# The first layer norm and the first two FFN chunks in two halves of 256 tokens

## The reference, cut to what matters

```python
        x = layer_norm(ALPHA * x + y @ w_out[l], ln_mix_g[l], ln_mix_b[l])
        hg, hu = jnp.split(x @ w_ffn_in[l], 2, axis=-1)
        x = layer_norm(ALPHA * x + (jax.nn.silu(hg) * hu) @ w_ffn_out[l], ln_ffn_g[l], ln_ffn_b[l])
```

## Time and profile before

| what | before |
|---|---|
| median of 3 runs | 861.37 us (860.73 to 861.94) |
| the profiled execution, its own time | 860.42 us |
| its span, first to last instruction | 858.6 us |
| TensorE busy | 835.9 us, 97% of the span |
| VectorE, ScalarE, GpSimd busy | 505.4, 347.7, 31.4 us |
| loads | 84.5 MB, 98 GB/s over the span |
| mean granted TensorE clock | 0.992 of full speed |

### The profile page before, as it was taken

How to read it: one execution, slowest core, us unless ns; L and a number is a source line. 1 busy time by engine, 2 the same in 40 slices (tenths; PEclk the granted TensorE clock), 3 DMA queues, 4 the chain that set the end, 5 groups by cost and what they waited for, 6 DMA issues and landing times.

```text
span 858.6 us, 10360 instructions
## 1 busy us (share of the span) xinstructions
PE 835.9 (97%) x3975; PEld 695.9 (81%) x3975; DVE 505.4 (59%) x831; ACT 347.7 (41%) x527; POOL 31.4 (4%) x81
## 2 busy tenths in 40 slices
PE   7999999999999999999999899999999999999995
PEld 4889898888887888888888688888888888888884
DVE  4357888888788987766553686333433333322227
ACT  4545566675645546534341632222222222211112
POOL 2600000000000000000000100000000000000001
PEclk9999999999999999999999999999999999999998
DMA  6552221212121221212253123322222222222202
GB/s 221 172 198 69 80 98 53 95 50 89 59 84 64 98 82 66 97 57 92 98 201 142 50 98 126 119 98 98 98 98 98 98 98 99 98 98 98 98 0 98
DMA packets 14680, 84.50 MB, mean 98 GB/s; under 512 B 1696, under 2 KB 2724, under 8 KB 5936
## 3 DMA queue, kind: packets, MB, share of 16 engines
q1 hardware_dynamic: 12480, 76.83, 24.8%
q0 software_dynamic: 2016, 6.86, 2.4%
q10 hardware_dynamic: 144, 0.26, 0.1%
HBM read 81.82 MB, written 2.13 MB: 98 GB/s over the span
## 4 chain that ended last, share of the span: by engine, by line
PE 84%; DVE 11%; ACT 2%; issue 1%; DMA 1%; POOL 0%; SPq 0%; DVEq 0%; POOLq 0%; ACTq 0%
PE bank L1181 57%; PE bank L1352 17%; PE bank L1311 2%; DVE w_lo L786 1%; PE bank L1218 1%; PE bank L1275 1%; DVE sel L863 1%; PE bank L1277 1%; ACT w_hi L500 1%; DVE top L861 1%; PE bank L1298 1%; PE bank L1410 1%; DVE pT_lo_D L891 1%; DMA xraw<-in_xT 1%; PE bank L1204 1%
## 5 line engine op out<-in xcount | busy, mean ns | idle before, releaser
L786 DVE TENSOR_TENSOR w_lo<-raw,w_hi 128x2048 fp32r<-128x2048 f32 x68 | 155.8, 2290 | 150.4 <-ACT w_hi L500 127.7
L1181 PE MATMUL bank<-x_lo,w_hi 128*128 128x512 f32 x720 | 183.8, 393 | 0.0
L1181 PE MATMUL bank<-x_hi,w_hi 128*128 128x512 f32 x720 | 179.4, 391 | 0.0
L1181 PE MATMUL bank<-x_hi,w_lo 128*128 128x512 f32 x720 | 178.4, 389 | 0.0
L1181 PEld LDWEIGHTS bank<-x_hi,w_lo 128*128 128x128 f32 x720 | 135.0, 188 | 28.1
L1181 PEld LDWEIGHTS bank<-x_lo,w_hi 128*128 128x128 f32 x720 | 134.5, 189 | 27.2
L1181 PEld LDWEIGHTS bank<-x_hi,w_hi 128*128 128x128 f32 x720 | 134.0, 188 | 27.5 <-DVE w_lo L786 0.3
L500 ACT ACTIVATE w_hi<-raw 128x2048 fp32r<-128x2048 f32 x47 | 90.2, 1918 | 107.4 <-PE bank L1352 94.9
L1352 PE MATMUL bank<-w_hi,h_hi 128*128 128x512 f32 x176 | 56.8, 389 | 0.0
L1352 PE MATMUL bank<-w_lo,h_hi 128*128 128x512 f32 x176 | 56.8, 389 | 0.0
L1352 PE MATMUL bank<-w_hi,h_lo 128*128 128x512 f32 x176 | 56.7, 389 | 0.0
(11 more groups left out here) (279 smaller groups left out, 1054.1 us busy)
## 6 DMA issues: line engine op xcount, KB each, us to landing
raw<-in_stream SPq DMA_DIRECT2D x68, 1024.0 KB, 4.8
resid<-in_x POOLq DMA_DIRECT2D x1, 2048.0 KB, 8.2
xraw<-in_xT SPq DMA_DIRECT2D x3, 512.0 KB, 7.3
out<-result SPq DMA_DIRECT2D x3, 512.0 KB, 2.6
raw<-in_stream SPq DMA_DIRECT2D x2, 512.0 KB, 8.2
bias_b<-bias_vectors POOLq DMA_DIRECT2D x1, 1024.0 KB, 6.3
bias_a<-bias_vectors POOLq DMA_DIRECT2D x1, 1024.0 KB, 10.6
ln_g<-in_g POOLq DMA_DIRECT2D x2, 512.0 KB, 7.7
```

What stands on the lines that cost most here:

```text
L786: dve.tensor_tensor(w_lo[:, s, :], raw[:, s, :], w_hi[:, s, :].bitcast(f32), ALU.subtract).then_inc(lo_ready, 1)
L1181: ins = pe.matmul(dst, lhs[a](k), rhs[b](k), start=n == 0, stop=n == n_all - 1)
```

## The change

All tensors that follow the norm are cut by tokens: `HALF[0]` is tokens 0 to 255 (tiles 0 and 1), `HALF[1]` the others.

- TensorE turns tiles 0 and 1 (`turn(0)`) ahead of the last 24 products of the output projection, into banks 0 to 3, two feature blocks of 256 tokens to a bank. Tiles 2 and 3 (`turn(1)`) go to banks 4 to 7, behind the gate chunk of the first half. Only that second turn waits for `mean_ready` of all tiles.
- Both chunks of the first pair are multiplied in halves by `x1_tiles(which, half)`, in the order gate half 0, turn(1), up half 0, gate half 1, up half 1. Each is 48 products of 256 tokens in place of 48 of 512 for both halves together.
- The turned first chunk: the early `x_lo` blocks (0 to 3) are multiplied before `w_lo`, which is waited for only at the 25th product.
- `x1t`, `x_hi` and `x_lo` are made in 16 pieces of 128x256 each, and stand at new places in the lists of VectorE and ScalarE. VectorE does `refine(0, 1)` ahead of `row_means` of tile 2, and the first half's pieces stand around `row_means` of tile 3 and `low(FIN0)`. ScalarE does `norm(1)` before `square(0, 2)`.
- `low(FIN0 + 1)` stands before the second half's `x1t` on VectorE, and `high(FIN0 + 1)` before its `x_hi` on ScalarE.

```diff
@@ ScalarE
+            def x1_high(half, first, end):
+
+                for k in range(first, end):
+                    act.wait_ge(x1t_ready, KT * half + k + 1)
+                    act.activation(x_hi[:, k, HALF[half]], x1t[:, k, HALF[half]], ACT.Copy).then_inc(x1_hi_ready, 1)
+
             square(0, 0)
             square(0, 1)
             norm(0)
+            norm(1)
             square(0, 2)
-            norm(1)
+            x1_high(0, 0, KT // 2)
             high(FIN0)
+            norm(2)
+            x1_high(0, KT // 2, KT)
             square(0, 3)
-            norm(2)
             norm(3, D_MODEL // 2)
...
                 if first:
                     high(FIN0 + 1)
+                    x1_high(1, 0, KT)
@@ VectorE
+            def x1_turned(half):
+
+                for k in range(KT):
+                    dve.wait_ge(turned, 4 * half + k // 2 + 1)
+                    first = SEQ // 2 * (k % 2)
+                    dve.tensor_scalar(x1t[:, k, HALF[half]], banks[4 * half + k // 2][:, first:first + SEQ // 2], g1_col[:, k:k + 1],
+                                      b1_col[:, k:k + 1], ALU.mult, ALU.add).then_inc(x1t_ready, 1)
...
+            row_means(mix_done, 0)
+            row_means(mix_done, 1)
+            refine(0, 0)
+            refine(0, 1)
+            row_means(mix_done, 2)
+            dve.wait_ge(cols_loaded, 32)
+            x1_turned(0)
+            refine(0, 2)
+            x1_low(0, 0, KT // 2)
+            row_means(mix_done, 3)
             low(FIN0)
+            x1_low(0, KT // 2, KT)
             refine(0, TOK - 1)
...
                 low(2 * p + (FIN0 + 1), (FIN0 + 1) % 2)
+                if first:
+                    x1_turned(1)
+                    x1_low(1, 0, KT)
@@ TensorE
+            def turn(half):
+
+                for tok in (2 * half, 2 * half + 1):
+                    pe.wait_ge(norm_ready, tok + 1)
+                    if half:
+                        pe.wait_ge(mean_ready, TOK)
...
+                    if before_last is not None and j == n_chunks - 2 and tok == TOK - 1:
+                        before_last()
...
+            def x1_tiles(which, half):
+
+                w = [columns((FIN0 + which) % 2, P * j, P, CW) for j in range(2)]
+                early, late = range(KT // 2), range(KT // 2, KT)
+                steps = ([(0, 0, k) for k in range(KT)] + [(0, 1, k) for k in early] + [(1, 0, k) for k in range(KT)]
+                         + [(0, 1, k) for k in late])
+                for n, (a, b, k) in enumerate(steps):
+                    pe.wait_ge(x1_lo_ready if b else x1_hi_ready, KT * half + k + 1)
+                    if n == 0:
+                        pe.wait_ge(hi_ready, FIN0 + which)
+                    if n == KT + KT // 2:
+                        pe.wait_ge(lo_ready, FIN0 + which)
...
+                if first:
+                    x1_tiles(0, 0)
+                    turn(1)
+                    x1_tiles(1, 0)
+                    x1_tiles(0, 1)
+                    x1_tiles(1, 1)
+                    return
```

More of the change, by code:

```diff
@@ L76 @@
 MASK_SLOT = 22
+HALF = [slice(0, SEQ // 2), slice(SEQ // 2, SEQ)]
 O_BUF = {"D": 0, "B": 1, "C": 0, "A": 1}
@@ L1084, in _, with x1_low @@
             dve.wait_ge(resid_loaded, 16)
-            for tok in range(TOK):
-                row_means(mix_done, tok)
-                if tok:
-                    refine(0, tok - 1)
+            def x1_turned(half):
[4 more added lines that the diff above has]
+                                      b1_col[:, k:k + 1], ALU.mult, ALU.add).then_inc(x1t_ready, 1)
+            def x1_low(half, first, end):
+                for k in range(first, end):
+                    dve.wait_ge(x1_hi_ready, KT * half + k + 1)
+                    dve.tensor_tensor(x_lo[:, k, HALF[half]], x1t[:, k, HALF[half]], x_hi[:, k, HALF[half]].bitcast(f32),
+                                      ALU.subtract).then_inc(x1_lo_ready, 1)
+            row_means(mix_done, 0)
[8 more added lines that the diff above has]
+            row_means(mix_done, 3)
             low(FIN0)
+            x1_low(0, KT // 2, KT)
             refine(0, TOK - 1)
@@ L1345, in _, with rows_product @@
                     slot_half(t, 1)
-            def rows_product(c0, n_chunks, left, chunk_signal, done, left_ready, first_banks_free):
+            def turn(half):
[3 more added lines that the diff above has]
+                        pe.wait_ge(mean_ready, TOK)
+                    for k in range(KT):
+                        if tok == TOK - 1 and k == KT // 2:
+                            pe.wait_ge(norm_half_ready, 1)
+                        first = SEQ // 2 * (k % 2) + P * (tok % 2)
+                        ins = pe.transpose(banks[4 * half + k // 2][:, first:first + P], resid[:, tok, P * k:P * (k + 1)], ident[:])
+                        if tok % 2 and k % 2:
+                            ins.then_inc(turned, 1)
+            def rows_product(c0, n_chunks, left, chunk_signal, done, left_ready, first_banks_free, before_last=None):
                 def tile(j, tok, kk, n, half):
@@ L1400, in ffn_pair @@
-            def ffn_pair(p, parity, first=False, early=False):
+                         lambda: pe.wait_ge(act_emptied, EMPTIED_BY.count("act")), lambda: turn(0))
+            def x1_tiles(which, half):
[9 more added lines that the diff above has]
+                        pe.wait_ge(lo_ready, FIN0 + which)
+                    for j in range(2):
+                        if n == 0 and half == 0:
+                            pe.wait_ge(x1t_ready, 2 * (2 * which + j + 1))
+                        ins = pe.matmul(banks[2 * which + j][:, HALF[half]], w[j][a](k), (x_hi, x_lo)[b][:, k, HALF[half]],
+                                        start=n == 0, stop=n == len(steps) - 1)
+                        if half and n == len(steps) - 1:
+                            ins.then_inc((gate_done, up_done)[which], 1)
@@ L1401, in ffn_pair @@
+            def ffn_pair(p, parity, first=False, early=False):
+                if first:
[5 more added lines that the diff above has]
+                    return
                 for which, signal, freed in ((0, gate_done, gated), (1, up_done, hidden_ready)):
                     pe.wait_ge(lo_ready, 2 * p + (FIN0 + which))
-                    if first and which == 0:
-                        w = [columns(FIN0 % 2, P * j, P, CW) for j in range(2)]
-                        for k in range(KT):
-                            pe.wait_ge(x1_hi_ready, k + 1)
-                            for a, j in ((0, 0), (1, 0), (0, 1), (1, 1)):
-                                if k == 0 and a == 0:
-                                    pe.wait_ge(x1t_ready, j + 1)
-                                pe.matmul(banks[j][:], w[j][a](k), x_hi[:, k, :], start=k == 0 and a == 0, stop=False)
-                        for j in range(2):
-                            for k in range(KT):
-                                pe.wait_ge(x1_lo_ready, k + 1)
-                                ins = pe.matmul(banks[j][:], w[j][0](k), x_lo[:, k, :], start=False, stop=k == KT - 1)
-                            ins.then_inc(signal, 1)
-                        continue
```

21 lines of the change are left out of this document (removed).

## The result

| what | before | after |
|---|---|---|
| median, runs taken together | 861.05 us (860.12 to 861.94, 6 runs) | **856.91 us** (855.03 to 857.82, 6 runs) |
| ratio, 95% interval | | 0.9949 [0.994, 0.9959] |
| the profiled execution, its span | 860.42, 858.6 us | 857.62, 855.8 us |
| mean granted clock of that execution | 0.992 | 0.990 |

The sign was right, the size was not.

What follows compares the result with a forecast made beforehand. TensorE bounds the kernel; in the stretch 475.95 to 512.21 us, 32.1 us of work, waits 1.0 + 0.4 and handovers 0.1 to 0.2 give 33.6 to 33.7 instead of 36.3. Gain 2.6, median 858.8 us, range 857.2 to 860.6.

Steps and rivals of the forecast that it cites:

- 5.4 us are waits, and these are all that the change can win: TensorE from 475.95 to 512.21 us: 30.8 us of work in 36.3, so only the 5.4 of waits can be won.
- 16 turns at the start of the stretch, no wait: turn(0) on TensorE at 475.95 us: norms of tiles 0 and 1 ready in time, slack 0.9; turns take 1.8 us.
- a short product: Pair 0's 192 products of 256 tokens: 0.120 us each, 23.0 us instead of 21.8, so the cut costs 1.3.
- `x_hi` 4 to 7 just in time, `w_lo` later: Gate chunk, half 0: TensorE loses 0.1 us to x_hi blocks, then waits for w_lo until 487.1; about 1.0 in all.
- norm of tile 3 within `turn(1)`: Second turn: tile 3's norm ready at 490.0 to 490.8 us while TensorE turns tile 2, so no wait.
- `w_hi` of `FIN0 + 1`: Ahead of up chunk, half 0: TensorE waits 0 to 0.8 us for ScalarE's w_hi; 0.4 taken.
- handovers: Pair 0 on TensorE: the more numerous handovers cost 0.1 to 0.2 us.
- pair 1's two `w_lo` after G: G ends the gate's second half; w_lo ready at G + 5.4 and G + 16.2, wanted at G + 5.8 and G + 16.7.
- rival (a): Better cover: short pieces cost half, GpSimd gets in early; gain 3.1 to 4.2 us, 857.2 to 858.3; chance 0.11.
- (b): VectorE's list becomes the bound through dearer pieces; gain only 0.6 to 1.9 us, 859.5 to 860.8; chance 0.19.
- (c): The 192 short products lose their pace: slower from 0.136 us each, 863.6 us at 0.145; chance 0.05.
- (d): No early start: turn(0) waits for norm(1), or pair 1 for its w_lo; 861.4 us if it takes all; chance 0.04.

Runs made afterwards that it cites:

- after_again: The changed kernel, unedited, in a second set of runs: 857.39 us against 861.65 for the kernel before, ratio 0.9945.
- filled_hi_early: Changed kernel with 17 unread products in TensorE's wait at the start, and high(FIN0 + 1) ahead of norm(3) on ScalarE: 856.46 us, ratio 0.9944.
- pair1_halves: The changed kernel with pair 1 too in products of 256 tokens, 192 instead of 96 of 512: 858.44 us, ratio 0.9965.
- turn_late: The changed kernel with turn(0) after the last 24 products of the output projection instead of ahead of them: 863.2 us, ratio 1.0021.
- before_all_filled: The kernel before with 17 unread products at its start and unread identity turns in TensorE's gaps of the norm: 858.43 us, ratio 0.9975.
- before_filled: The kernel before with 17 unread products of 512 columns in TensorE's wait at the start: 859.62 us, ratio 0.9974.
- whole_chunks: The changed kernel with norm, turns and pieces in halves, but the first two chunks multiplied whole, behind turn(1): 862.27 us, ratio 1.0007.
- order_undone: The changed kernel, still in halves, but with w_hi and w_lo by turns for each block as before: 861.51 us, ratio 0.9995.

## Why the prediction was wrong in size and right in sign

**The step that failed** is "5.4 us are waits, and these are all that the change can win". It held for the profiled execution and was carried over to the median as if every execution were like it. Five of six traces of before have another cost at the same place: after the four gaps the clock falls, and the first gate products run at half pace, for 0.93 to 1.65 us. The change removes all but 0.4 us of the gaps, and none of its six traces has the fall. So the sum lacked a term, put at nothing without a reason: what the clock costs behind the waits, 0.94 us in the mean of six traces. The forecast set the median from the trace by adding 0.95 us (861.37 less 860.42) to both kernels, as if the change could not touch it; by the traces most of it was the cost that the change takes away. (That 0.94 and 0.95 agree so closely is luck, since the executions also differ in the start and near 262 us.) Of the 1.9 us between 858.8 and 856.91, this term is 0.9, and 0.7 are mis-sized terms of the stretch, below. The other 0.2 or 0.3 are within the scatter of a set: `after_again` came to 857.39, inside the range.

There were two signs of it in the numbers at hand. The profiled execution lay below all three timed runs (860.42 against 860.73 to 861.94); of the 52 runs of before that were timed later, only 5 took 860.5 us or less. And its clock, 1.00 in the stretch, had fallen elsewhere in the same trace behind waits of TensorE: to 0.91 over the first 20 us, and near 262 us behind a wait of 2.0.

**Point by point**, for the quick traces, where 3.33 us were won and 2.6 forecast:

| step | forecast | measured | |
|---|---|---|---|
| 16 turns at the start of the stretch, no wait | 1.8 us | 1.67 | right; 0.105 a turn, not 0.113: 0.3 less for 32 |
| the 24 products of tile 3 | 5.44 | 5.53 | right; 0.09 is a handover |
| a short product | 0.120 us | 0.120 | exact; cost 1.3 |
| `x_hi` 4 to 7 just in time, `w_lo` later | 1.0 us | 0.29 + 0.56 | right in both place and size |
| `w_lo` of `FIN0` ready, after the start of the stretch | 11.1 | 10.8 | right |
| norm of tile 3 within `turn(1)` | no wait | none | right |
| `w_hi` of `FIN0 + 1` | 0.4 us | 0.04 | too dear by 0.36 |
| handovers | 0.15 | 0.23 | too cheap by 0.08 |
| pair 1's two `w_lo` after G (503.62) | 5.4, 16.2 | 5.3, 16.1 | covered, by 0.5 and 0.6 |

How some of these are read: 483.65 to 485.86 is 2.21 us for a sixteen that takes 1.92, hence 0.29. From 485.86 to 487.38 is 1.52 for an eight of 0.96, hence 0.56. For `w_hi` the turn takes 1.70 (490.33 to 492.03), and 1.66 in `filled_hi_early`, where `w_hi` is made early. The handovers are what the first products behind a turn or a wait take more than their like: 0.09 in the 24 products of tile 3, 0.07 in each of the sixteens from 487.38 and 492.03 (1.99 instead of 1.92). The `w_lo` rows end at 508.9 and 519.7.

Of the mis-sized terms the largest is the wait ahead of the up chunk. The bounds were 0 and 0.8, by whether GpSimd gets in between VectorE's `x_lo` pieces, and I took the middle. It got in: `var_eps` ended with `w_lo` (487.28), the power took 0.61 within the four `x_lo`, and `shift` was there at 489.28, the early end. Of rival (a) this half was true. The other half, short pieces at half the price, was not: `x1t` stands 0.45 us apart and `x_lo` 0.335, as counted.

Of the rivals, (b) did not occur: nothing on VectorE's list was dearer than taken by more than 0.01 us apiece. (c) is refuted by `pair1_halves`. (d) did not occur, but `turn_late` prices it: 863.2 us rather than 861.4, since a late start also shifts `w_hi`, and the clock falls.

**What stays open.** What decides whether the clock falls and for how long (0.93 to 1.65 us in before, with gaps of the same lengths) no run tells. The Trainium skill (TensorE: Matmul & The Clock Gate, "What's actually happening") says that the chip's observation is not tied to the kernel's start, which would let the same gaps meet it differently from one execution to the next; the traces are in line with it but don't prove it. Nor does a run tell why the fall near 262 us was absent in two of 17 traces, or what filling the gaps by itself is worth: `before_all_filled` and `before_filled` would have to be timed side by side, with several traces of each.

## What to carry to other kernels

Work that needs only part of the operands, placed before what the others are waiting for, is worth more than the wait it fills: it can also keep TensorE's clock up behind the wait. Before a time is forecast from one trace, look whether that execution is like the others: one whose time lies below all the timed runs may lack a cost that most have. And cutting the pieces is worth nothing by itself; what wins is the order in which the consumer takes them (`whole_chunks`, `order_undone` and `turn_late` each keep most of the change and lose all of the gain).

## What the runs showed of the hardware

- Short gaps are enough. 1.04, 0.44, 1.76 and 0.92 us of idleness within 8 us took the clock from 2.4 to 1.2 GHz in five of six executions (in one of them ahead of the last gap); products of 512 then stand 0.43 us apart instead of 0.227 for 3 to 4.4 us. In `order_undone`, `turn_late` and `whole_chunks` single waits of 3.3 to 3.9 us did the same, and a single wait of 2.0 us near 262 us did it in 15 of 17 traces, at 1.56 us.
- A gap filled with work that nobody reads is worth something: with 17 products in the wait at the start the clock of the first 20 us was 1.00 instead of 0.91 or 0.83, and the work at 50 us began 0.95 and 1.13 us earlier. What 27 turns in the gaps of before are worth was not shown.
- GpSimd's power on one column took 0.55 us alone, 0.61 between short instructions of VectorE, 1.41 under one long one.
- Products of 256 columns cost 0.120 us against 0.227 for 512, although each weight load is drawn 0.192 us long: as drawn, the loads overlap one another as well as the products.
